# Feed-forward stages: turning the gated activations with VectorE squares and GpSimd transfers in place of TensorE

## What is computed

```
def swiglu(x, w_gate, w_up, w_down):
    return (jax.nn.silu(x @ w_gate) * (x @ w_up)) @ w_down

x = x + 0.5 * swiglu(rms_norm(x, ffn1_norm[layer]), ffn1_w_gate[layer], ffn1_w_up[layer], ffn1_w_down[layer])
```

## Time and profile before

| | us |
|---|---|
| median of 3 runs | 2624.53 (2624.11 to 2626.18) |
| the profiled execution | 2624.62 |
| its span, first to last instruction | 2622.8 |
| TensorE busy | 2583.5 (99%) |
| VectorE busy | 1876.2 (72%) |
| ScalarE busy | 1182.2 (45%) |
| GpSimd busy | 136.5 (5%) |

### The profile page before, as it was taken

The page is one execution under the profiler, slowest core; times in us unless marked ns, Lnnn a source line. Parts: engine busy times, 40 slices in busy tenths (PEclk is TensorE's granted clock), DMA queues, the critical chain, the costliest instruction groups (busy, mean ns, idle before and its releaser), DMA issues.

```text
span 2622.8 us, 31939 instructions
## 1 busy us (share of the span) xinstructions
PE 2583.5 (99%) x12175; PEld 2141.9 (82%) x12175; DVE 1876.2 (72%) x2263; ACT 1182.2 (45%) x1611; POOL 136.5 (5%) x133
## 2 busy tenths in 40 slices
PE   8999999999999999999999999999999999999998
PEld 6888888878888888888888888888888888878887
DVE  7986358889873599844556998449984469799843
ACT  6444236664443454432225544335443337654431
POOL 0000004500000000000000000000000044100000
PEclk9999999999999999999999999999999999999999
DMA  5332332133313333223333432243332321243222
GB/s 176 118 105 69 95 89 79 33 118 116 113 61 95 119 116 109 76 85 97 97 96 114 128 105 77 81 132 98 111 89 81 97 87 41 88 122 104 77 85 81
DMA packets 221944, 252.87 MB, mean 96 GB/s; under 512 B 8928, under 2 KB 157152, under 8 KB 221792
## 3 DMA queue, kind: packets, MB, share of 16 engines
q1 hardware_dynamic: 221792, 250.81, 31.6%
HBM read 248.68 MB, written 2.10 MB: 96 GB/s over the span
## 4 chain that ended last, share of the span: by engine, by line
PE 88%; DVE 7%; ACT 2%; issue 2%; SPq 0%; DMA 0%; DVEq 0%; POOLq 0%; POOL 0%; ACTq 0%
PE pair L536 28%; PE pair L538 28%; PE pair L540 28%; PE pair L663 2%; DVE wl L1592 2%; PE pair L764 1%; DVE Sl L1602 1%; DVE Sf L1602 1%; DVE Xl L1602 0%; DVE acc L1602 0%; ACT Qf L1161 0%; DVE part L1579 0%; ACT wh L1130 0%; DVE X L1602 0%; PE pair L840 0%
## 5 line engine op out<-in xcount | busy, mean ns | idle before, releaser
L1592 DVE TENSOR_TENSOR wl<-raw,wh 128x1024 fp32r<-128x1024 f32 (+2 forms) x547 | 648.5, 1188 | 437.0 <-ACT wh L1130 435.1
L1130 ACT ACTIVATE wh<-raw 128x1024 fp32r<-128x1024 f32 (+2 forms) x547 | 563.0, 1030 | 741.3 <-PE pair L540 717.2
L538 PE MATMUL pair<-Hl,wh 128*128 128x512 f32 (+1 forms) x1061 | 428.8, 404 | 0.0
L536 PE MATMUL pair<-Hh,wl 128*128 128x512 f32 (+1 forms) x1061 | 419.7, 396 | 0.0
L540 PE MATMUL pair<-Hh,wh 128*128 128x512 f32 (+1 forms) x1061 | 419.0, 395 | 0.0
L536 PE MATMUL pair<-wh,Xl 128*128 128x512 f32 (+2 forms) x976 | 375.6, 385 | 17.7 <-ACT Xh L1161 7.1
L536 PE MATMUL pair<-wh,Sl 128*128 128x512 f32 x960 | 376.0, 392 | 5.2 <-DVE wl L1592 5.2
L540 PE MATMUL pair<-wh,Sh 128*128 128x512 f32 x960 | 375.7, 391 | 0.0
L538 PE MATMUL pair<-wl,Sh 128*128 128x512 f32 x960 | 375.7, 391 | 0.0
L538 PE MATMUL pair<-wl,Xh 128*128 128x512 f32 (+2 forms) x976 | 373.7, 383 | 0.0
L540 PE MATMUL pair<-wh,Xh 128*128 128x512 f32 (+2 forms) x976 | 373.7, 383 | 0.0
(11 more groups left out here) (322 smaller groups left out, 3403.9 us busy)
## 6 DMA issues: line engine op xcount, KB each, us to landing
raw<-in_ffn_w_gate SPq DMA_DIRECT2D x120, 512.0 KB, 4.4
raw<-in_ffn_w_up SPq DMA_DIRECT2D x120, 512.0 KB, 3.7
raw<-in_ffn_w_down SPq DMA_DIRECT2D x114, 512.0 KB, 3.5
raw<-in_c_w_in SPq DMA_DIRECT2D x24, 512.0 KB, 3.8
raw<-in_w_in SPq DMA_DIRECT2D x10, 512.0 KB, 3.8
raw<-in_a_w_in SPq DMA_DIRECT2D x8, 512.0 KB, 3.7
raw<-in_a_w_out SPq DMA_DIRECT2D x8, 512.0 KB, 3.4
raw<-in_c_w_out SPq DMA_DIRECT2D x8, 512.0 KB, 3.4
```

The source lines that it names most:

```text
L536: e.matmul(o, ll, rh, start=start, stop=False, skip_group_check=again)
L538: e.matmul(o, lh, rl, start=False, stop=False, skip_group_check=again)
L1130: e.activation(part_of(n, wh), source_of(n), ACT.Copy).then_inc(whi.up(("w", n)), 1)
L1592: e.tensor_tensor(part_of(n, wl), source_of(n), part_of(n, wh).bitcast(F), ALU.subtract).then_inc(wlo.up(("w", n)), 1)
```

## The change

Blocks 16 to 19 (group 4) are still turned by TensorE, beside blocks 13 to 16 of the first down pass. The other 18 blocks are turned in two steps. First VectorE transposes within squares of 32x32 (`turn_squares`, one instruction of 128x512 for each block, four for each group), from `H` into a free place: the squares of group 0 into blocks 8 to 11 of `H`, those of group 1 into 12 to 15, of group 2 into 16 to 19, of group 3 into `squares3` (in the place of `Sh[2]` and `Sl[2]`), those of the rest into blocks 14 and 15. Then GpSimd issues 16 transfers for each set (`move_blocks`), one for each pair of partition quarters, which bring the squares to their places in `H`; the sets go in the order 0, rest (4), 1, 2, 3. ScalarE and VectorE then make `Hh` and `Hl` from `H` and no longer from a PSUM bank.

VectorE's new instructions stand in groups 1 to 3 after steps 2 and 3 (two blocks each; the squares of the group before), in group 1 also after step 4 (the rest), and in group 4 after steps 5 and 6 (those of group 3). New waits: VectorE waits for the rest's transfers before the squares of set 1 and, at step 8 of groups 2, 3 and 4, for the sets whose squares lie where it writes next; ScalarE waits for a set's transfers before its high halves and for set 3 before block 8. `begins` is returned by the planner and not read.

```diff
+        turned_in = [Event(sem(f"turned_in{q}")) for q in range(5)]
...
+        squares3 = at("squares3", [128, 4, 4, 128], F, 45056 + 16384)
+
+        def squares(q):
+
+            return squares3[:, :, :, :] if q == 3 else H[:, 4 * q + 8:4 * q + 12, :, :]
+
+        def block_moves(s, m):
+
+            spans = [slice(32 * i, 32 * i + 32) for i in range(4)]
+            for j in spans:
+                for i in spans:
+                    if m < 4:
+                        yield H[j, 4 * m:4 * m + 4, :, i], squares(m)[i, :, :, j]
+                    else:
+                        whole = (FFN[s][0] - GROUPED - j.start + 127) // 128
+                        yield H[j, 20:20 + whole, :, i], H[i, 14:14 + whole, :, j]
...
-            def turn_hidden(s, *ks):
-
-                for k in ks:
-                    rows = last_block(s) if k == 21 else 128
-                    bank = take(turn_bank(s, k), ("turn", s, k))
-                    w.wait_ge(par_in, 16)
-                    w.wait_ge(dve, ("h", s, k // 4))
-                    for t in range(4):
-                        src = H[:, k, t, :] if k < 20 else Hrest[:, t, 128 * (k - 20):128 * (k - 20) + rows]
-                        e.transpose(bank[0:rows, 128 * t:128 * t + 128], src, ident).then_inc(mm.up(("turn", s, k)), 1)
-                        yield
+            def turn_hidden(s, k):
+
+                bank = take(turn_bank(s, k), ("turn", s, k))
+                w.wait_ge(par_in, 16)
+                w.wait_ge(dve, ("h", s, 4))
+                for t in range(4):
+                    e.transpose(bank[:, 128 * t:128 * t + 128], H[:, k, t, :], ident).then_inc(mm.up(("turn", s, k)), 1)
+                    yield
...
-                    product(s, g, take_pair(x, ("E2", s, g)), "E2", Sh[3], Sl[3], 0, 0, False,
-                            turn_hidden(s, 0, 1, 2) if g == 4 else iter(()))
+                    product(s, g, take_pair(x, ("E2", s, g)), "E2", Sh[3], Sl[3], 0, 0, False)
...
-                            turned = turn_hidden(s, k + 3) if t0 == 0 and k + 3 < 22 else iter(())
+                            turned = turn_hidden(s, k + 3) if t0 == 0 and 16 <= k + 3 < 20 else iter(())
...
                 rows = last_block(s) if k == 21 else 128
-                w.wait_ge(mm, ("turn", s, k))
                 if 16 <= k < 20:
+                    w.wait_ge(mm, ("turn", s, k))
                     w.wait_ge(wlo, ("grouped", s))
-                copy(Hh(k)[0:rows, :], banks[turn_bank(s, k)][0:rows, :], ("hh", s, k))
+                    copy(Hh(k), banks[turn_bank(s, k)][:, :], ("hh", s, k))
+                else:
+                    w.wait_ge(mm, (("D", "B", "E", "E2", None, "E2")[k // 4], s, 4))
+                    w.wait_ge(turned_in[min(k // 4, 4)], ("turned", s, min(k // 4, 4)))
+                    if k == 8:
+                        w.wait_ge(turned_in[3], ("turned", s, 3))
+                    copy(Hh(k)[0:rows, :], H[0:rows, k, :, :].rearrange("p t q -> p (t q)"), ("hh", s, k))
...
+            def turn_squares(s, m, *ks):
+
+                w.wait_ge(dve, ("h", s, m))
+                if m == 1:
+                    w.wait_ge(turned_in[4], ("turned", s, 4))
+                if m == 3:
+                    w.wait_ge(mm, ("E", s, 4))
+                for k in ks:
+                    e.transpose(squares(m)[:, k, :, :], H[:, 4 * m + k, :, :]).then_inc(dve.up(("squares", s, m)), 1)
+
+            def turn_rest_squares(s, n):
+
+                w.wait_ge(dve, ("h", s, 5))
+                for k, cols in ((14, 128), (15, n - 128)):
+                    at0 = 128 * (k - 14)
+                    e.transpose(H[:, k, :, 0:cols], Hrest[:, :, at0:at0 + cols]).then_inc(dve.up(("squares", s, 4)), 1)
...
+                            for m in {2: (0,), 3: (1, 4), 4: (2,)}.get(g, ()):
+                                w.wait_ge(turned_in[m], ("turned", s, m))
                             tt(hidden(g, 2), blocks(x), blocks(U3), ALU.add, ("C22", s, g), ("read", ("E", s, g)))
...
+                        if u in (2, 3) and 0 < g < 4:
+                            turn_squares(s, g - 1, 2 * u - 4, 2 * u - 3)
+                        if u in (5, 6) and g == 4:
+                            turn_squares(s, 3, 2 * u - 10, 2 * u - 9)
+                        if u == 4 and g == 1:
+                            turn_rest_squares(s, f - GROUPED)
...
+            def move_blocks(s, m):
+                w.wait_ge(dve, ("squares", s, m))
+                for dst, src in block_moves(s, m):
+                    e.dma_start(dst, src).then_inc(turned_in[m].sem, 16)
+                    turned_in[m].n += 16
+                turned_in[m].also(("turned", s, m))
...
             for s in range(1, 10):
                 {2: mixer_mla, 5: mixer_conv, 8: mixer_fnet}.get(s, norm)(s)
+                if s in FFN:
+                    for q in (0, 4, 1, 2, 3):
+                        move_blocks(s, q)
                 pool.also(("end", s))
```

More of the change, by code:

```diff
@@ L164, in plan @@
     loads, units, release = [], [], []
+    begins = {}
     holder, ring = {}, {}
@@ L187, in plan @@
         s, first, blocks = c
+        begins.setdefault(s, []).append(u)
         if first and s in AFTER_MIXER:
@@ L206, in plan @@
                 unit(512, 2, range(N_RING), 3, source, total)
-    return loads, units, release, sums
+    return loads, units, release, sums, begins
 def weight_stream(a):
@@ L307, in build @@
         ident = col("ident", 0, 128)
-        loads, units, release, sums_before = plan(weight_stream(a))
+        loads, units, release, sums_before, begins = plan(weight_stream(a))
         stage_at = -(-(stage_base - 128) // 256) * 256 + 128
@@ L688, in rest, with product @@
                         hooks.pop(0)()
-            def product(s, g, into, name, lh, ll, kh0, column, start, between=iter(())):
+            def product(s, g, into, name, lh, ll, kh0, column, start):
                 for kh in range(2):
@@ L702, in product @@
                             mm3(into[:, i, :], lh[:, k, sl], ll[:, k, sl], h[:, kk, :], l[:, kk, :],
-                                start and kh == 0 and kk == 0, end, *names, again=not start, between=between if kh else iter(()))
+                                start and kh == 0 and kk == 0, end, *names, again=not start)
             def ffn(s):
@@ L1677, in hidden_low @@
                 rows = last_block(s) if k == 21 else 128
-                bank = banks[turn_bank(s, k)]
                 dst = Hl[:, k, :] if rows == 128 else Hh(k)[rows:2 * rows, :]
                 w.wait_ge(act, ("hh", s, k))
-                if k == 20:
-                    w.wait_ge(mm, ("turn", s, 21))
-                tt(dst, bank[0:rows, :], Hh(k)[0:rows, :].bitcast(F), ALU.subtract, ("hl", s, k), ("read", ("turn", s, k)))
+                if 16 <= k < 20:
+                    tt(dst, banks[turn_bank(s, k)][:, :], Hh(k).bitcast(F), ALU.subtract, ("hl", s, k), ("read", ("turn", s, k)))
+                else:
+                    w.wait_ge(turned_in[min(k // 4, 4)], ("turned", s, min(k // 4, 4)))
+                    tt(dst, H[0:rows, k, :, :].rearrange("p t q -> p (t q)"), Hh(k)[0:rows, :].bitcast(F), ALU.subtract,
+                       ("hl", s, k))
+            def turn_squares(s, m, *ks):
[11 more added lines that the diff above has]
+                    e.transpose(H[:, k, :, 0:cols], Hrest[:, :, at0:at0 + cols]).then_inc(dve.up(("squares", s, 4)), 1)
             def gate(s, g, first):
```

2 lines of the change are left out of this document (added).

## The result

The changed kernel takes 2953.94 us (median, 2951.09 to 2955.09), the kernel before 2624.32 in the same comparison; the ratio is 1.125 (95% interval 1.1238 to 1.1265). I had forecast 2576 with a range of 2568 to 2889. The time lies beyond both, on the side of rival (1).

The account below looks back on a forecast made before the run. TensorE was taken as the bound, busy 2583.5 of 2622.8 us. 2624.6 less 51.6 for removed transposes gave 2573.0; with VectorE's and GpSimd's work hidden and 3 us for leads, 2576, range 2568 to 2889.

Parts of the forecast that it names:

- rival (1): GpSimd needs over 1.1 us per transfer, so VectorE's wait in group 2 stops TensorE; 2679 to 2889 us; chance 0.40.
- What is removed: On TensorE, 432 of 528 transposes go, at 0.1195 us each: 51.6 us saved.
- its allowance for leads: 3 us added to 2573.0, half a microsecond per FFN, for leads that shrink to near nothing.
- VectorE's squares: 18 square transposes of 128x512 per FFN on VectorE, 0.60 us each, costing nothing while the 4.4 us lead lasts.
- rival (3): VectorE becomes the bound at 1.22 us per square transpose: 35 us in all, 2608 us; chance 0.05.
- The price of a transfer in GpSimd's queue: Each of 80 transfers per FFN takes GpSimd 1.0 us, with bounds of 0.37 and 2.3 us.
- The two deadlines: Rest's transfers before set 1's squares in group 2, set 3 before block 8: room 35.4 and 26.9 us, no stall.
- Sets 1 and 2 have some 50 us each: The transfers of these two sets have that much time, so no stall was booked for them.
- DMA load, booked at nothing: Transfer pieces take 16 to 69 us of each DMA engine per 345 us FFN; no cost booked.
- The clock after a stop: A stopped TensorE may come back at a lower clock level, as at the kernel's end (granted 0.80); no time booked.
- (2): VectorE shuts GpSimd out, leaving it only VectorE's idle time to write transfers; 360 us, 2933 us; chance 0.07.
- the serial end of (1): One transfer in flight at 2.3 us each: 52.7 us stall per FFN, 316 us in all, 2889 us.

Follow-up runs that it names:

- the kernels with other room: The changed kernel with only `dynamic_dma_scratch_size` raised from 1024, to 1536, 2048 or 2816: 2693.63, 2615.94 and 2594.06 us.
- the kernel with the rest early: The changed kernel, 1024 bytes kept, with the rest's squares turned after step 7 of group 0 and its transfers issued first: 2842.47 us, ratio 1.083.

## Why the prediction was wrong, step by step

- **What is removed**: right. 96 transposes are left of 528, and without the transfers' waits the kernel stands at 2575.8 where the prediction had 2573.0, or 2576 with its allowance for leads.
- **VectorE's squares**: right. They cost 688 ns, 0.61 us from start to start (two in 1.31), against 0.60 taken and 0.49 to 1.22 as bounds; rival (3) fell with that. The lead hid 1.8 us (30.68 against 28.92), against 2.0.

```profile
L1717 DVE STREAM_TRANSPOSE H<-H 128x512 f32<-128x512 f32 x72 | 46.8, 688 | 179.8 <-DMA H<-H 179.8
...
L680 PE MATMUL pair<-par,H 128*128 128x128 f32 x96 | 26.0, 271 | 0.0
```

- **The price of a transfer in GpSimd's queue**: here the forecast failed. I took 1.0 us from GpSimd's least compute step. What an engine needs for a compute step says nothing about how many transfers it may have under way. The time GpSimd is busy, 0.65 us, lies even below it; the wait for room makes it 2.37. The upper bound, "if each has to wait for the one before", was the mechanism that came, and with its 2.3 us nearly its size. In the first FFN the 32 transfers took 61.8 us from the first start to the last (93.8 to 155.6), the second half of them at half the size, where 35.4 us were to hold them and the last landing.
- **The two deadlines**: the places are right, and so is the form of the sum. At its own upper bound it gives 52.7 us of stop per FFN; the trace has 333.2/6 = 55.5. But that is two errors against each other. The rest's transfers were booked as whole ones; they are half ones in threes, 17.8 us for the sixteen where 16 x 2.3 is 36.8, so the first stop is 28.9 us in place of 40.5. Against it, the second stop is 21.6 us in the first FFN in place of 12.2, since set 3 starts behind set 2 (its squares are done at 248.0, its first transfer starts at 255.6), and the weight loads stretch it. The rest of the 55.5 is stops at step 8, the next point.
- **"Sets 1 and 2 have some 50 us each"**: wrong. The room to step 8 is some 45 us, set 1 needs 48 to 52 (its first transfer to its last, in the six FFNs), and the two waits make 11.8 us per FFN on VectorE, which reach TensorE mainly in one stop of 3.1 to 4.2 us.
- **DMA load, booked at nothing**: wrong for the transfers, right for the loads, whose median landing is 4.3 us for the gate weights (4.4 before). In the engines' shares it is small: the transfers took 3.9% of the span, 19 us of each engine per FFN, near the lower end of the 16 to 69 us of the prediction. But at one in flight each transfer's own landing stands on the path, and a weight load in the same DMA engines makes 2.37 us into 3 to 4.8. About 24 us per FFN.
- **The clock after a stop**: named and not priced; 45 us in all, 7.6 us per FFN, after short stops as after long ones. Without it the time would be 2909, still beyond the range.
- **Rivals.** (1) came, with its place, its sign and its mechanism "one in flight", and was given 0.40; the kernels with other room lie around its break-even of 1.30 us per transfer: at 1.26 us undisturbed the time is 0.3% under that of before, at 1.53 it is 2.6% over. That it fits so well is in part luck, for beside loads those transfers take longer, and the rest's take less. (2) would have given 2933, nearer to the measured time than any other figure, and its mechanism, which no row of the kernel before showed, is refuted all the same: GpSimd's distances do not follow VectorE. A time that fits does not show a cause.
- **The range** ended at 2889 because I took the serial end of (1) with deadlines independent and loads and clock at nothing. Those three are what it lacked. They do not simply add up: the 24 us of the loads hold a part of the clock's 7.6 and of the queue's share, and against them stand the rest's transfers, booked 19 us per FFN too dear (36.8 against 17.8).

## What to carry to other kernels

Price a transfer issued by GpSimd by how many may be in flight, not by its issue: here 1, 2, 3 and 5 of 64 KB at a `dynamic_dma_scratch_size` of 1024, 1536, 2048 and 2816, that is one for every 512 to 563 (estimated from these counts). At one in flight each cost a whole landing, 2.37 us from start to start where GpSimd was busy for 0.65, and the weight loads beside it lengthened that: 2.88 us with whole loads, 2.54 with an eighth of their bytes. Where an engine waits at several places for one queue, write that queue's times out from the first transfer to the last against all deadlines together, and compare its length per turn with the length of the turn. Raise that number, where the kernel lets you, before the moves are blamed: here 2816 in place of 1024 and the rest's squares and transfers moved earlier turned 12.5% lost into 1.7% won.

## What the runs showed that I had not expected

- GpSimd waits for its whole batch: with five in flight it does not issue the sixth when the first has landed, but 1.75 us after the fifth was issued. In the second row of the kernel with 2816 bytes above, each of the five lands 2.1 us after its own start: the first at 222.8, before the fifth is even issued, the last at 225.4, and the next five begin at 225.76. Where transfers of 32 KB follow one of 64 KB, though, eight go in a row with 2048 bytes (from 118.89, 4.68 us), the last 64 KB one among them, where the table has seven of 32 KB. So how room is given back stays open; only how many of one size fit is shown.
- GpSimd and SyncE need about the same to issue a transfer of 512 pieces, 0.65 and 0.74 us; a weight load, of larger pieces, takes SyncE 0.37.
- TensorE's granted clock was 0.50 for 3 to 6 us after stops of 21.5 to 31.3 us, and likewise around six stops of only 3.1 to 4.2 us, then full again. Eighteen such stops cost 45 us. In the kernel with the rest early, six long stops and more short ones left TensorE busy for just as long, 2579.8 us.
